# A hybrid decoder trunk on one core: keys and values of the memory as three products of word pairs, and another order at the start, between the layers and at the end

## The chip, the cores and the metric

The kernel runs on one core of a Trainium2 chip. Its time is the device time of one launch in microseconds (us), as the median of several runs. The profile shows one execution. The engines are TensorE (PE, its weight loads PEld), VectorE (DVE), ScalarE (ACT), GpSimd (POOL) and SyncE (SP), which issues most transfers. Each has its own queue of instructions, in program order; they wait for one another by semaphores.

## The reference

Two layers over 512 prompt tokens and 8 single-token samples, 1024 channels, fp32. Each layer normalises `x`, makes one wide projection `h @ w_in`, feeds three branches, and adds `m @ w_out`. The branches are a complex state space (S5), a causal depthwise convolution of 31 taps, and an attention into 256 memory rows. What the change touches is the last one's keys and values, and the norms:

```python
def mem_kv(mem, g, w_k, w_v):
    hm = rmsnorm(mem, g)
    k = (hm @ w_k).reshape(bsz, N_MEM, N_XHEADS, XHEAD_DIM)
    v = (hm @ w_v).reshape(bsz, N_MEM, N_XHEADS, XHEAD_DIM)
    return k, v

h = rmsnorm(x, p['norm_g'])                       # each layer
s_new = ...                                       # powers of exp(lam * dt), a scan over positions
prob = softmax(q k^T * scale); o_x = prob @ v
x = x + m @ p['w_out']
...
y_prompt = rmsnorm(xp, final_norm_g); y_sample = rmsnorm(xs, final_norm_g)
```

## The kernel before

The tokens lie along the free axis: `xT` holds 8 tiles of 128 channels by 520 columns (512 tokens and 8 samples, in two halves of 260). A wide product is not made in fp32. Each operand is split in two fp32r words, a high one and the rest, and three matmuls of 260 columns are added up in PSUM (`split_product`, L785): w_hi by h_hi, w_lo by h_hi, w_hi by h_lo. SP loads the weights in half-units into four slots `w_st`; ACT casts a slot to `w_hi` (L1209), POOL subtracts it from the raw weights to make `w_lo` (L658). A layer has 72 units, in a fixed order: `v0`, `v1`, `q0`, `q1` and so on up to `out`. `first_pair` (L813) makes the first two units together, since it takes each tile of `h` as it comes.

The order on every engine is written out by hand. At the head of a layer DVE makes `ht` from `xT`, the gain and `rs`; ACT casts it to `h_hi` (L1249); DVE subtracts to make `h_lo` (L1692). `rs` is 1/rms as a row over all partitions. In layer 0 it comes from diagonal matrices `dg` that DVE makes (L1668) and PE multiplies by ones (`row_factors`, L755). In layer 1 DVE sums the squares of the new `x` tiles (`add_square`), PE sums over the channels (`square_sums`, L836), DVE takes a reciprocal (L1687), ACT a root.

The keys and values are `key_values`: fp32 matmuls of 128x512, 32 a layer, of the raw weights `wkv` (3 places, loaded two row tiles at a time) and the normalised, gained memory `memg` (L828). Their outputs lie in `mp`; ACT copies the keys to `ktok` and PE turns them to `kT`. They are made in pieces between the turns of the tokens in layer 0, and around `first_pair` in both layers.

Meanwhile DVE computes powers of the state matrix, many operations of 128x16 (`step_factors`, `first_powers`, `chunk_powers`; helper lines L1540, L1556), and then starts the taps of the convolution (`convolution`, first row L1735). Among these it serves the attention: `scores_max` (L1716), and the probabilities' scaling by the reciprocal of their sum (L1723 and `pr<-pr,stat`), for one quarter of the tokens at a time. PE turns the first quarter's probabilities (L709, `mp<-ident,pr`) amid its products; this is the first place behind the layer's head at which PE needs DVE's late work. `state_turns` turn the sample states and the C matrices; DVE copies them to `s0` and `cT` (L1704, L1706).

The end of the program, behind the last product: PE turns `xT` back to rows, ACT squares them with a sum, DVE takes the reciprocal, ACT the root, DVE scales the rows from PSUM by that and the gain row `grow`, SP stores them.

Of the kernel before, what the change touches and what calls it, by code (L numbers as in the profile page):

```python
# [15 lines left out]
F32 = mybir.dt.float32  # L16
# [56 lines left out]
def build(nc, x_prompt, x_sample, mem_prompt, state_ssm_re, state_ssm_im, state_conv, cache_mem_k,  # L73
# [12 lines left out]
    with ctx:  # L86
# [8 lines left out]
        w_dir = sb("w_dir", [P, 2, 12 * P])  # L95
        q = sb("q", [P, ET, 2, HC])
# [6 lines left out]
        dcol = sb("dcol", [P, 4])  # L103
# [37 lines left out]
        def rr(name, off, shape):  # L141
# [13 lines left out]
        drow = ur("drow", 1024, [4, P])  # L155
        dtrow = ur("dtrow", 1040, [80, 2])

# [11 lines left out]
        memg = rr("memg", 6272, [P, KT, MEM])  # L169
# [16 lines left out]
        dg = zr("dg", 2048, [P, 4, P])  # L186
        dgs = zr("dgs", 2560, [NB, NB])
        sq = rr("sq", 0, [P, KT, 2, HC])
        ht = rr("ht", 9216, [P, 2, 2, HC])
        rs = rr("rs", 10256, [P, 2, HC])  # L190
# [33 lines left out]
        grow = rr("grow", 8320, [P, D])  # L224
        ysr = rr("ysr", 9344, [NB, D])
        xsc = rr("xsc", 10368, [P, KT, NB])

# [22 lines left out]
            x_in0 x_in1 xs_in mem_in consts x_tr x_ev dg_done rs_done mem_nrm mem_ev mem_out g_in fin_tr  # L250
            row_sq row_var row_rt fin_y fin_out""".split()}
# [8 lines left out]
            rstd_done=1 ht_done=8 hhi_done=8 h_done=8 par_tr=3 par_ev=3 memg_done=8  # L260
            kv_used=8 kv_ev=2 kT_tr=1 kT_ev=1 kv_out=32 q_ev=4 dt_exp=1 sin_arg=1 par_act=1 sc_done=4
# [73 lines left out]

        block = ctx.enter_context(nc.Block())
# [3 lines left out]
        def _(sp):  # L340
            def param_loads(l):
# [13 lines left out]
                sp.dma_start(drow[:, :], ssm_d[l].rearrange("(q x) -> q x", x=P)).then_inc(sm["p_in"], 16)  # L355
# [27 lines left out]
            for l in range(LAYERS):  # L383
# [20 lines left out]
                def kv_load(i):  # L404

                    src = (w_k, w_v)[i // 4][l].rearrange("(k p) c -> p k c", p=P)
                    if i >= 3:
                        wait(sp, l, "kv_used", i - 2)
# [3 lines left out]
                if l:  # L412
                    kv_load(0)
                    kv_load(1)
                pair("v0")
                if l:
                    kv_load(2)
                else:
                    state_loads(0)
                    kv_load(3)  # L420
                pair("v1")
                for i in range(3 if l else 4, 6):
                    kv_load(i)
                half("q0", 0)
                kv_load(6)
                half("q0", 1)
                kv_load(7)
                half("q1", 0)

# [185 lines left out]
                for j in range(KT):  # L615
# [7 lines left out]
                    if j == 2:  # L623
                        residual_load(1)

# [6 lines left out]
            sp.dma_start(grow[:, :], final_norm_g.rearrange("(o d) -> o d", o=1).to_broadcast([P, D])).then_inc(sm["g_in"], 16)  # L632
# [11 lines left out]
        def _(pool):  # L644
# [7 lines left out]
            for l in range(LAYERS):  # L652
# [49 lines left out]
                for n in range(unit["tail"], UNITS):  # L702
                    low(l * UNITS + n)
# [1406 lines left out]
```

## Time and profile before

| | before |
|---|---|
| time, median of 3 runs | 1102.6 us (1098.14 to 1104.03) |
| the profiled execution | 1097.4 us, of which the span is 1095.6 us |
| mean granted clock of TensorE | 0.990 |
| PE busy | 1057.8 us, 97% of the span |
| DVE busy | 804.3 us, 73% |
| ACT busy | 439.4 us, 40% |
| POOL busy | 405.0 us, 37% |

The span reaches from the first instruction to the last. Busy times are sums over instructions, and the ends of matmuls are modelled, so that rows of PE overlap: a matmul's row is a good deal longer than the step to the next one. What counts is where each engine waits, and for whom; the shares above say nothing of that.

### The profile page before, as it was taken

The numbers are of one execution on the slowest core, as the hardware profiler recorded it, in microseconds if no ns is written. First come the engines' busy times: TensorE is split into PE (matmuls) and PEld (weight loads), VectorE is DVE, ScalarE is ACT, GpSimd is POOL, SyncE is SP. The second block draws the span as 40 slices with busy tenths as digits, with TensorE's granted clock in tenths as the row PEclk, the third lists the DMA queues.
The fourth block names the chain that finished last, engine by engine and source line by source line (L and its number), as shares of the span: only waits on it lengthen the run. The fifth ranks groups of instructions, "written<-read, shape, count | busy, mean of one in ns | idle before, by whom it ended". The sixth has DMA issues, their size and how long they took to land.

```text
span 1095.6 us, 20431 instructions
## 1 busy us (share of the span) xinstructions
PE 1057.8 (97%) x8226; PEld 989.5 (90%) x8226; DVE 804.3 (73%) x1221; ACT 439.4 (40%) x825; POOL 405.0 (37%) x329
## 2 busy tenths in 40 slices
PE   6899999999999999999999999999999999999995
PEld 3669998989999989999966999898999998999994
DVE  3899879898988784444588987989898978544413
ACT  5333653435453352222433355334446346222222
POOL 0135443343342324444412544344443332344440
PEclk8999999999999999999999999999999999999998
DMA  9336519973326933444532562696442694344422
GB/s 266 99 97 173 193 51 206 249 190 98 116 60 152 221 105 120 133 131 159 152 117 78 155 215 67 145 293 171 121 128 59 140 181 148 117 127 136 136 78 78
DMA packets 225268, 155.01 MB, mean 141 GB/s; under 512 B 48650, under 2 KB 201674, under 8 KB 223110
## 3 DMA queue, kind: packets, MB, share of 16 engines
q1 hardware_dynamic: 219318, 141.52, 47.4%
q10 hardware_dynamic: 5856, 12.19, 3.4%
q8 instruction: 65, 1.06, 0.4%
q14 instruction: 29, 0.24, 0.1%
HBM read 130.38 MB, written 24.24 MB: 141 GB/s over the span
## 4 chain that ended last, share of the span: by engine, by line
PE 78%; DVE 11%; DMA 4%; ACT 3%; issue 2%; SPq 1%; POOL 1%; DVEq 0%; ACTq 0%
PE acc L785 54%; PE mp L1132 11%; PE mp L828 3%; PE mp L709 2%; PE mp L1037 1%; PE mp L1005 1%; PE mp L1030 1%; PE mp L896 1%; PE mp L934 1%; DMA w_st<-in_w_br_xatt 1%; DVE br_lo L1814 1%; DVE br_hi L1813 1%; PE acc L813 1%; DVE ht L1546 1%; DVE tiny L1540 1%
## 5 line engine op out<-in xcount | busy, mean ns | idle before, releaser
L658 POOL TENSOR_TENSOR w_lo<-w_st,w_hi 128x512 fp32r<-128x512 f32 x288 | 385.8, 1344 | 608.9 <-ACT w_hi L1209 605.4
L785 PE MATMUL acc<-h_hi,w_hi 128*128 128x260 f32 x1600 | 457.9, 286 | 0.0
L785 PE MATMUL acc<-h_hi,w_lo 128*128 128x260 f32 x1600 | 451.9, 282 | 0.0
L785 PE MATMUL acc<-h_lo,w_hi 128*128 128x260 f32 x1600 | 451.6, 282 | 0.0
L1209 ACT CAST w_hi<-w_st 128x512 fp32r<-128x512 f32 x288 | 178.0, 622 | 358.7 <-PE acc L785 191.2
L785 PEld LDWEIGHTS acc<-h_hi,w_hi 128*128 128x128 f32 x1600 | 301.1, 188 | 7.2 <-issue 3.6
L785 PEld LDWEIGHTS acc<-h_hi,w_lo 128*128 128x128 f32 x1600 | 301.3, 188 | 0.7 <-issue 0.5
L785 PEld LDWEIGHTS acc<-h_lo,w_hi 128*128 128x128 f32 x1600 | 301.4, 188 | 0.0
L1546 DVE SCALAR_TENSOR_TENSOR acc<-vx,cw,acc 128x512 f32<-128x512 f32 x240 | 181.4, 756 | 9.8
L1132 PE MATMUL mp<-br_hi,w_hi 128*128 128x260 f32 x384 | 78.0, 284 | 5.2 <-DVEq L2016 5.2
L1132 PE MATMUL mp<-br_lo,w_hi 128*128 128x260 f32 x384 | 77.4, 283 | 0.0
L1132 PE MATMUL mp<-br_hi,w_lo 128*128 128x260 f32 x384 | 77.2, 283 | 0.0
L785 PE MATMUL acc<-m_hi,w_hi 128*128 128x260 f32 x256 | 69.7, 282 | 0.0
L785 PE MATMUL acc<-m_hi,w_lo 128*128 128x260 f32 x256 | 69.6, 282 | 0.0
L785 PE MATMUL acc<-m_lo,w_hi 128*128 128x260 f32 x256 | 69.6, 282 | 0.0
L1540 DVE TENSOR_TENSOR mj<-mp,xT 128x520 f32<-128x520 f32 x16 | 11.2, 700 | 76.7 <-PE mp L1132 75.8
L1132 PEld LDWEIGHTS mp<-br_hi,w_hi 128*128 128x128 f32 x384 | 59.2, 188 | 6.1 <-issue 6.0
L828 PE MATMUL mp<-wkv,memg 128*128 128x512 f32 x128 | 61.5, 635 | 2.5 <-DVE memg L1640 2.3
L1132 PEld LDWEIGHTS mp<-br_hi,w_lo 128*128 128x128 f32 x384 | 59.3, 188 | 0.0
L1132 PEld LDWEIGHTS mp<-br_lo,w_hi 128*128 128x128 f32 x384 | 59.2, 188 | 0.0
L828 PEld LDWEIGHTS mp<-wkv,memg 128*128 128x128 f32 x128 | 25.2, 203 | 33.0 <-issue 30.0
L1540 DVE TENSOR_TENSOR X<-X,s 128x16 f32<-128x16 f32 (+9 forms) x88 | 51.5, 585 | 3.0
(305 smaller groups left out, 1392.9 us busy)
## 6 DMA issues: line engine op xcount, KB each, us to landing
w_st<-in_w_in SPq DMA_DIRECT2D x208, 256.0 KB, 3.2
g_scratch<-xT ACTq DMA_DIRECT2D x32, 260.0 KB, 2.3
xT<-g_scratch SPq DMA_DIRECT2D x8, 1040.0 KB, 7.4
kb<-in_cache_mem_k SPq DMA_DIRECT2D x16, 512.0 KB, 4.6
kb<-in_cache_mem_v SPq DMA_DIRECT2D x16, 512.0 KB, 6.8
w_st<-in_w_out SPq DMA_DIRECT2D x32, 256.0 KB, 2.8
x_scratch<-xT SPq DMA_DIRECT2D x2, 2080.0 KB, 8.5
xT<-x_scratch SPq DMA_DIRECT2D x4, 1040.0 KB, 5.6
```

What stands on the lines that cost most here:

```text
L658: pool.tensor_tensor(w_lo[:, slot, :], w_st[:, slot, :], w_hi[:, slot, :].bitcast(F32), ALU.subtract).then_inc(w_staged_free, 1)
L709: return pe.transpose(out, in_, ident[0:n, 0:n])
L785: last = pe.matmul(bank(l, i + b), w[:, slot, kk * P:(kk + 1) * P], x[:, k, b, :], start=(k == 0 and p == 0), stop=(k == KT - 1 and p == 2))
L813: last = pe.matmul(bank(l, 2 * i + a), w[:, c % SLOTS, kk * P:(kk + 1) * P], x[:, k, a, :], start=(k == 0 and p == 0), stop=(k == KT - 1 a ...
L828: last = pe.matmul(mp[:, 2 * (1 - i // 4) + m, :], memg[:, k, m * P:(m + 1) * P], wkv[:, i % 3, kk * E:(kk + 1) * E], start=(k == 0), stop ...
L896: last = pe.matmul(mp[:, 2 * (i % 2) + hd // 2, (hd % 2) * MEM:(hd % 2 + 1) * MEM], q[:, hd, i // 2, (i % 2) * P:(i % 2 + 1) * P], kT[:, h ...
L934: last = pe.matmul(mp[:, hd, :], vtok[:, m, hd * P:(hd + 1) * P], pT[:, hd, m, :], start=(m == 0), stop=(m == 1))
L1005: last = pe.matmul(mp[:, 2 * h + e, (r % 4) * YC:(r % 4 + 1) * YC], wl[:, r, e, :], U[:, f * QH + r, e, NB:UC], start=True, stop=True)
L1132: last = pe.matmul(mp[:, 2 * jj + a, 0:HC], w[:, slot, c0:c0 + P], y[:, x, k, a, :], start=(k == 0 and i == 0), stop=(k == ET - 1 and i == 2))
L1209: act.copy(w_hi[:, c % SLOTS, :], w_st[:, c % SLOTS, :]).then_inc(w_hi_done, 1)
L1540: run(dve.tensor_tensor(out, a, b, op), behind)
L1546: run(dve.scalar_tensor_tensor(out=out, in0=a, scalar=s, in1=b, op0=op0, op1=op1), behind)
```

## The change

**Keys and values.** `memg` becomes two words, `mg_hi` (DVE in layer 0, ACT in layer 1) and `mg_lo` (DVE, `memory_low`). The weights become two words a row tile: `key_high` on ACT makes the high word in one of three places `wk[l][n % 3]`, when the products have left it, and `key_low` on POOL the low one. `key_values` counts 16 blocks n of one row tile, with 6 matmuls of 512 columns each, fp32r. **Order.** `state_turns` move from before `first_pair` to between the halves of `v1`, and their copies on DVE behind the first convolution call. `dg` is made by ACT. `step_factors` of layer 0 move behind the h words; `first_powers((1, 2))` of layer 1 move from output unit 6 to behind the last square sum. There are three `ht` buffers, and no wait for the end of each operation in that loop. ACT's `sines(0)` stand before the h casts. **End.** The final gain is a column scale by ACT on `xT` tiles (`gained`); the turns of finished tiles (`final_turns`) stand inside the output units of layer 1, five a unit; ACT keeps raw rows; the squares are summed by PE (`square_rows`); DVE scales rows 0 to 2, ACT row 3 and the samples; ACT issues some of the stores.

```diff
                 def key_values(first, end):
-                    for i in range(first, end):
-                        wait(pe, l, f"d_loaded{i % 3}", 16 * (i // 3 + 1))
-                        for kk in range(2):
-                            k = 2 * (i % 4) + kk
-                            wait(pe, l, "memg_done", k + 1)
-                            for m in range(2):
-                                last = pe.matmul(mp[:, 2 * (1 - i // 4) + m, :], memg[:, k, m * P:(m + 1) * P],
-                                                 wkv[:, i % 3, kk * E:(kk + 1) * E], start=(k == 0), stop=(k == KT - 1))
+                    for n in range(first, end):
+                        k = n % KT
+                        wait(pe, l, "memg_done", k + 1)
+                        wait(pe, l, "wk_done", n + 1)
+                        if l and n == KT:
+                            wait(pe, l, "var_done", 1)
+                        for m in range(2):
+                            for p, (x, w) in enumerate(((mg_hi, 0), (mg_lo, 0), (mg_hi, 1))):
+                                last = pe.matmul(mp[:, 2 * (1 - n // KT) + m, :], x[:, k, m * P:(m + 1) * P],
+                                                 wk[l][n % 3][:, w, :], start=(k == 0 and p == 0), stop=(k == KT - 1 and p == 2))
                         last.then_inc(sm["kv_used"], 1)
...
+            def key_high(l, first, end):
+                for n in range(first, end):
+                    if n % 2 == 0:
+                        wait(act, l, f"d_loaded{n // 2 % 3}", 16 * (n // 6 + 1))
+                    if n >= 3:
+                        wait(act, l, "kv_used", n - 2)
+                    act.copy(wk[l][n % 3][:, 0, :], wkv[:, n // 2 % 3, (n % 2) * E:(n % 2 + 1) * E]).then_inc(sm["wk_hi_done"], 1)
...
+                def key_low(first, end, l=l):
+                    for n in range(first, end):
+                        wait(pool, l, "wk_hi_done", n + 1)
+                        pool.tensor_tensor(wk[l][n % 3][:, 1, :], wkv[:, n // 2 % 3, (n % 2) * E:(n % 2 + 1) * E],
+                                           wk[l][n % 3][:, 0, :].bitcast(F32), ALU.subtract).then_inc(sm["wk_done"], 1)
...
                 if l == 0:
-                    key_values(0, 1)
+                    wait(pe, 0, "par_ev", 1)
+                    key_values(0, 2)
                     token_turns(0)
                     token_turns(1)
                     sample_turns()
-                    key_values(1, 2)
+                    key_values(2, 4)
                     token_turns(2)
                     token_turns(3)
-                    key_values(2, 3)
+                    key_values(4, 6)
                     row_factors()
-                    key_values(3, 4)
+                    key_values(6, 8)
                     pe.wait_ge(sm["x_ev"], 5)
+                    key_values(8, 10)
                 else:
-                    key_values(0, 2)
+                    key_values(0, 4)
                     square_sums()
-                    key_values(2, 4)
-                state_turns()
+                    key_values(4, 12)
                 first_pair()
-                wait(pe, l, "par_ev", 3)
-                key_values(4, 8)
+                key_values(12 if l else 10, 16)
...
-                pair("v1")
+                one("v1", 0)
+                state_turns()
+                one("v1", 1)
...
-                            first_powers((1, 2))
+                            for k in range(KT):
+                                memory_low(l + 1, k, memn[:, k, :])
...
                     dve.sem_inc(sm["sq_sum"], 1)
+                    first_powers((1, 2))
```

On POOL at the seam between the layers, before, the weight words run on with nothing of the keys among them (`w_lo` are the low words of the weights):

```order
L658 TENSOR_TENSOR w_lo<-w_st,w_hi 128x512 x96
L678 MEMSET qrow 40x512
L658 TENSOR_TENSOR w_lo<-w_st,w_hi 128x512 x4
L670 TENSOR_TENSOR vx<-vx,sg 128x4x64 x2
L672 TENSOR_TENSOR v_s<-v_s,sg 128x8
```

Now sixteen subtractions of key words begin there, of which six are shown (the three `wk_` names are the three places):

```order
L668 TENSOR_TENSOR w_lo<-w_st,w_hi 128x512 x94
L690 TENSOR_TENSOR wk_10920_75<-wkv,wk_10920_75 128x512
L690 TENSOR_TENSOR wk_11944_76<-wkv,wk_11944_76 128x512
L690 TENSOR_TENSOR wk_5120_77<-wkv,wk_5120_77 128x512
L690 TENSOR_TENSOR wk_10920_75<-wkv,wk_10920_75 128x512
L690 TENSOR_TENSOR wk_11944_76<-wkv,wk_11944_76 128x512
L690 TENSOR_TENSOR wk_5120_77<-wkv,wk_5120_77 128x512
L668 TENSOR_TENSOR w_lo<-w_st,w_hi 128x512 x2
```

Blocks 0 to 5 of the keys went ahead of the last two weight words of the first pair; ten more blocks stand behind these two.

On DVE at the same place, before, the powers `pw` lie ahead of the last residual adds (`xT<-acc,xT`), and `rs` comes straight behind the last square sum:

```order
L1540 TENSOR_TENSOR pw<-pw 128x16x2
L1540 TENSOR_TENSOR pw<-tiny,pw 128x16x2
L1556 COPY pw<-tiny 128x16x2
L1540 TENSOR_TENSOR xT<-acc,xT 128x260 x2
L1540 TENSOR_TENSOR sq<-sq 128x520 x2
L69 ISA
L1543 TENSOR_SCALAR rs<-mp 128x520
L1687 RECIPROCAL rs<-rs 128x520
```

Now the eight `mg_lo` lie ahead of the adds, and the powers (14 operations, of which the first three and the last three are shown) between the sum and `rs`:

```order
L1772 SCALAR_TENSOR_TENSOR mg_lo<-memn,vec,mg_hi 128x256 x8
L1673 TENSOR_TENSOR xT<-acc,xT 128x260 x2
L1673 TENSOR_TENSOR sq<-sq 128x520 x2
L1673 TENSOR_TENSOR tiny<-pw 128x16 x2
L1673 TENSOR_TENSOR tiny<-tiny 128x16
```

```order
L1673 TENSOR_TENSOR pw<-pw 128x16x2
L1673 TENSOR_TENSOR pw<-tiny,pw 128x16x2
L1689 COPY pw<-tiny 128x16x2
L69 ISA
L1676 TENSOR_SCALAR rs<-mp 128x520
L1825 RECIPROCAL rs<-rs 128x520
```

The powers moved from ahead of `x`'s last tiles to between the last square sum and `rs`.

On ACT ahead of the h casts of layer 0, before (`tiny` are the sines' arguments):

```order
L1165 ACT_TABLE_LOAD
L1165 ACTIVATE tiny<-tiny 128x16
L1166 ACT_TABLE_LOAD
L1166 ACTIVATE tiny<-tiny 128x32
L1209 CAST w_hi<-w_st 128x512 x4
L1249 CAST h_hi<-ht 128x520 x8
```

and now, behind `dg`:

```order
L1282 ACTIVATE dg<-ident,stat 128x128 x4
L1283 ACTIVATE dgs<-ident,stat 8x8
L1245 CAST wk_0_72<-wkv 128x512
L1245 CAST wk_2048_73<-wkv 128x512
L1290 CAST w_hi<-w_st 128x512 x2
L1245 CAST wk_3072_74<-wkv 128x512
L1290 CAST w_hi<-w_st 128x512 x2
L1245 CAST wk_0_72<-wkv 128x512
L1230 ACT_TABLE_LOAD
L1230 ACTIVATE tiny<-tiny 128x16
L1231 ACT_TABLE_LOAD
L1231 ACTIVATE tiny<-tiny 128x32
```

Key casts, each of which waits for PE to leave a place, went between the weight casts, and the sines with their table loads behind them. Five more key casts stand at and among the h casts.

## Rows read from the trace of the kernel before

**Rows 1.** TensorE between the layers: start, us, line, operation, [idle before <-releaser].

```profile
552.70 7.03 PE L828 MATMUL mp<-wkv,memg 128*128 128x512 f32 x16
560.47 1.14 PE L836 MATMUL mp<-sq,ones 128*128 128x260 f32 x4 [0.74 <-DVEq L2062]
```

**Rows 2.** Windows: length, busy of PE PEld DVE ACT POOL, PEclk, DMA, GB/s.

```profile
36.00:40.00 4.00, 4.00 (x12) 2.07 (x11) 2.74 (x14) 0.00 (x0) 0.00 (x0) 0.64 0.93 272
540.00:550.00 10.00, 10.00 (x86) 10.00 (x86) 8.42 (x21) 6.15 (x12) 5.13 (x4) 1.00 0.42 129
```

**Rows 3.** TensorE's timeline in layer 0, where dg arrives.

```profile
35.28 1.13 PE L755 MATMUL acc<-dg,ones 128*128 128x128 f32 x8 [3.16 <-DVEq L1670]
...
36.88 5.40 PE L828 MATMUL mp<-wkv,memg 128*128 128x512 f32 x8
```

**Rows 4.** VectorE's timeline, small operations of the powers, layer 0's last units.

```profile
546.54 1.23 DVE L1540 TENSOR_TENSOR tiny<-tiny,vec 128x16 f32<-128x16 f32 x1
547.80 0.18 DVE L1540 TENSOR_TENSOR tiny<-pw,vec 128x16 f32<-128x16 f32 x1
```

**Rows 5.** GpSimd's timeline at the same place.

```profile
546.45 2.71 POOL L658 TENSOR_TENSOR w_lo<-w_st,w_hi 128x512 fp32r<-128x512 f32 x2 [1.11 <-ACT w_hi L1209]
```

**Rows 6.** VectorE's groups by line and form: count, busy, mean ns, idle.

```profile
L1540 DVE TENSOR_TENSOR mj<-mj,tj 128x520 f32<-128x520 f32 x32 | 42.8, 1337 | 5.8 <-DVE tj L1540 2.9
...
L1540 DVE TENSOR_TENSOR mj<-mp,xT 128x520 f32<-128x520 f32 x16 | 11.2, 700 | 76.7 <-PE mp L1132 75.8 <-DVE mj L1540 0.4 <-DVE br_lo L1814 0.4
```

**Rows 7.** VectorE's timeline in layer 0, up to the convolution's first row.

```profile
30.36 4.59 DVE L1668 TENSOR_SCALAR dg<-ident,stat 128x128 f32<-128x128 f32 x4
...
39.60 0.70 DVE L1682 COPY rs<-acc 128x520 f32<-128x520 f32 x1 [0.85 <-DVE tiny L1540]
...
52.68 1.55 DVE L1692 TENSOR_TENSOR h_lo<-ht,h_hi 128x520 fp32r<-128x520 f32 x2
54.37 0.42 DVE L1704 COPY s<-mp 128x256 f32<-128x256 f32 x1
...
73.06 0.19 DVE L1735 COPY v_last<-vx 128x32 f32<-128x32 f32 x1
```

**Rows 8.** ScalarE's timeline in layer 0, a table load and the first h cast.

```profile
27.81 1.28 ACT L1166 ACT_TABLE_LOAD   x1
...
41.19 0.63 ACT L1249 CAST h_hi<-ht 128x520 fp32r<-128x520 f32 x1 [9.78 <-DVEq L1699]
```

**Rows 9.** VectorE's timeline in layer 1: rs, and the convolution's first row.

```profile
561.65 0.70 DVE L1543 TENSOR_SCALAR rs<-mp 128x520 f32<-128x520 f32 x1 [1.29 <-PE mp L836]
...
596.17 0.19 DVE L1735 COPY v_last<-vx 128x32 f32<-128x32 f32 x1
```

**Rows 10.** TensorE's timeline: kT's and the probabilities' turns in both layers.

```profile
70.81 1.04 PE L709 MATMUL mp<-ident,ktok 128*128 128x128 f32 x8
...
127.19 1.03 PE L709 MATMUL mp<-ident,pr 128*128 128x128 f32 x8
...
596.50 1.04 PE L709 MATMUL mp<-ident,ktok 128*128 128x128 f32 x8
...
653.20 1.03 PE L709 MATMUL mp<-ident,pr 128*128 128x128 f32 x8
```

**Rows 11.** VectorE's timeline: the probabilities of head 0 in both layers.

```profile
124.78 1.22 DVE L1540 TENSOR_TENSOR pr<-pr,stat 128x1024 f32<-128x1024 f32 x1
...
650.79 1.23 DVE L1540 TENSOR_TENSOR pr<-pr,stat 128x1024 f32<-128x1024 f32 x1
```

**Rows 12.** VectorE's waits, 73 to 126 us, then 597 to 652: total, times, longest.

```profile
DVE stat L1723 <- ACT pr L1322: 0.3, 1, 0.3
...
DVE stat L1716 <- PE mp L896: 2.6, 2, 1.7
DVE stat L1723 <- ACT pr L1322: 1.3, 1, 1.3
```

**Rows 13.** VectorE's timeline at the end: the last residual add.

```profile
1076.46 0.43 DVE L1540 TENSOR_TENSOR xT<-acc,xT 128x260 f32<-128x260 f32 x1 [2.35 <-PE acc L785]
```

More of the change, by code:

```diff
@@ L624, in _ @@
                         residual_load(1)
+                    if j == 5 and l + 1 < LAYERS:
+                        wait(sp, l, "sfin_out", 64)
+                        for i in range(3):
+                            kv_load(i, l + 1)
                 wait(sp, l, "kv_out", 32)
@@ L758, in row_factors, with turn_samples, final_turns, square_rows @@
                 last.then_inc(sm["rs_done"], 1)
+            def turn_samples(k):
+                if k == HK:
+                    pe.wait_ge(sm["fin_kept"], HK + 1)
+                if k == KT - 1:
+                    pe.wait_ge(sm["fin_g"], KT + 2)
+                transpose(mp[0:NB, 2, (k % HK) * P:(k % HK + 1) * P], xsc[:, k, :], P).then_inc(sm["fin_tr"], 1)
+            def final_turns(k):
+                if k >= 2:
+                    pe.wait_ge(sm["fin_kept"], rows_kept(k - 2))
+                for i in range(4):
+                    if k < KT - 1 and i == 0:
+                        pe.wait_ge(sm["fin_g"], k + 1)
+                    if k == KT - 1 and i % 2 == 0:
+                        pe.wait_ge(sm["fin_g"], KT + i // 2)
+                    last = transpose(mp[:, k % 2, i * P:(i + 1) * P], xg[:, k % 2, i // 2, (i % 2) * P:(i % 2 + 1) * P], P)
+                last.then_inc(sm["fin_tr"], 1)
+                if k < KT - 1:
+                    turn_samples(k)
+            def square_rows(part):
+                wait(pe, LAYERS - 1, "sq_sum", part + 1)
+                for i in range(4):
+                    last = pe.matmul(mp[:, 3, 4 * i:4 * i + 4], sq[:, part * (KT - 1), i // 2, (i % 2) * P:(i % 2 + 1) * P],
+                                     ones[:, 0:4], start=(i == 0 and part == 0), stop=(i == 3 and part == 1))
+                if part:
+                    last.then_inc(sm["rs_done"], 1)
+            def sample_squares():
+                wait(pe, LAYERS - 1, "sq_sum", 3)
+                pe.wait_ge(sm["fin_kept"], rows_kept(KT - 2))
+                pe.matmul(mp[0:NB, 0, 0:4], sqs[:, :], ones[:, 0:4], start=True, stop=True).then_inc(sm["rs_done"], 1)
             memory_turns(0)
+            param_turns(0)
             memory_turns(1)
-            param_turns(0)
-            wait(pe, 0, "par_ev", 1)
             for l in range(LAYERS):
@@ L1202, in _ @@
             act.wait_ge(sm["row_rt"], 2)
-            sines(0)
+            act.wait_ge(sm["consts"], 3)
+            for i in range(4):
+                act.activation(dg[:, i, :], ident[:, :], ACT.Copy, scale=stat[:, 16 + i:17 + i])
+            act.activation(dgs[:, :], ident[0:NB, 0:NB], ACT.Copy, scale=stat[0:NB, 20:21]).then_inc(sm["dg_done"], 1)
+            key_high(0, 6, 7)
             for l in range(LAYERS):
@@ L1633, in add_square, with memory_low @@
                 tt(sq[:, 0, :, :], sq[:, 0, :, :], sq[:, k, :, :], ALU.add)
+            def memory_low(l, k, rows):
+                wait(dve, l, "mg_hi_done", k + 1)
+                dve.scalar_tensor_tensor(out=mg_lo[:, k, :], in0=rows, scalar=vec[:, 56 + k:57 + k], in1=mg_hi[:, k, :].bitcast(F32),
+                                         op0=ALU.mult, op1=ALU.subtract).then_inc(sm["memg_done"], 1)
             run(dve.memset(stat[:, 4:5], 1.0))
@@ L1665, in _ @@
             dve.sem_inc(sm["x_full"], 1)
-            dve.wait_ge(sm["row_rt"], 1)
-            for i in range(4):
-                run(dve.tensor_scalar(dg[:, i, :], ident[:, :], stat[:, 16 + i:17 + i], None, ALU.mult), behind=1)
-            run(dve.tensor_scalar(dgs[:, :], ident[0:NB, 0:NB], stat[0:NB, 20:21], None, ALU.mult))
-            dve.sem_inc(sm["dg_done"], 1)
-            step_factors(0)
             steps.clear()
```

259 lines of the change are left out of this document (166 added, 93 removed).

## The prediction

> **What bounds the kernel now.** The core's one granted clock is 0.990, so TensorE (PE) runs at 2.4 GHz almost throughout, and the place to start is its timeline at the seams between phases. Between the layers the last product is followed at once by the first half of the keys, 16 records in 7.03 us; the square sums behind them wait 0.74 us for VectorE (DVE) [rows 1]. So PE has hardly a gap there, and the key and value matmuls are time on the path. The windows give the pace of the split products: 86 matmuls of 260 columns in 10.00 us, 0.116 us each, at clock 1.00 [rows 2]. An fp32 matmul of the keys leaves two records, so it takes 2 x 0.44 = 0.88 us.
>
> Then I read what hands PE its work. Ahead of the first products of layer 0 PE idles 3.16 us for `dg`, and the same eight records then take 5.40 us and not 8 x 0.44 = 3.5: the windows show the granted clock at 0.64 there, that is, mostly at the 1.2 GHz level [rows 2, 3]. An idle PE costs twice: its gap, and here 1.8 us behind it.
>
> **A price the argument rests on.** GpSimd (POOL) subtracts words in ops of two SBUF inputs, two in 2.71 us. One DVE op of 128x16 that begins beside them takes 1.23 us; the one behind it takes 0.18 [rows 4, 5]. The groups by form say it of large ones: DVE's `mj<-mj,tj`, both inputs in SBUF, means 1.337 us, and `mj<-mp,xT` of the same size with one in PSUM 0.700 [rows 6]. So a POOL subtraction that meets DVE's two-input work costs DVE 1.23 - 0.18 = 1.05 us; I take 1.0, since some begin in gaps. The Trainium skill, "SBUF — State Buffer", section "Who interferes with whom", has it as an exclusive lock held for the whole instruction, whose loser fully blocks. The trace agrees in kind, and is a little cheaper in size; with a whole op lost each time the sum below would come out some 8 us later.
>
> **The change, part by part.**
> *The products.* 32 fp32 matmuls of 512 columns a layer (32 x 0.86 = 27.5 us; 7.03 / 8 = 0.88 with the ends) become 96 of fp32r. A 512-column one is not in the trace. From 0.116 for 260 columns it is 0.229, from half of a record of 0.43, 0.215; I take 0.22, 21.2 us. PE's work falls by 6.3 us a layer, if it is fed.
> *What feeds them.* Each of 16 blocks a layer now needs an ACT cast (0.6) and a POOL subtraction (1.3) before it, three in flight. POOL can supply a block each 1.3 us, and PE uses one in 6 x 0.22 = 1.3: no reserve. In layer 0 my ordering of the queues by these durations gives: keys end early, but blocks 8 and 9 come at 36.3 and 41.1, so PE idles there; the first pair of products runs from 42.5; block 15 ends at 63.1; `v1` starts at 64.0, where before it starts behind `kT` turns at 70.81 + 0.8 = 71.6 [rows 10]. PE is 7.6 us early.
> *DVE, layer 0.* `dg` goes to ACT (four scalings 4.59 us off DVE), `step_factors` goes behind the h words, so `rs` is copied at 30.3 and not 39.60 [rows 7]. But the h casts wait for ACT, which has key casts, weight casts and now both sines with their table loads of 1.28 us ahead of them: first `h_hi` at 36.5, before 41.19 [rows 8]. With the key casts put between them, the h words end at 52.9 (before 52.68 + 1.55 = 54.2), -1.3. Then: the two state copies moved away -1.1 (0.42 for the first, whose rows are half as long as the second's); `step_factors` now here +3.7; three and a part of a fourth POOL key subtraction (blocks 12 to 15), which now stand among powers, where POOL was idle or had only weight words, +3.4. The convolution, whose first op is `v_last` at 73.06 [rows 7], starts at 77.8: +4.7.
> *DVE, layer 1.* The square sum is complete at 560.4 as before, but `first_powers` now stands between it and `rs`. It is 14 small ops, 14 x 0.21 = 2.9 us, and eight POOL ops (key blocks 3 to 8 and two weight words) fall on it: +8.4. `rs` begins at 571.7, before 561.65 [rows 9]: +10.0. In the h loop the end-of-op waits are gone (-2.0), but ACT's key casts stand between the h casts and five POOL ops meet the words, +5.1: the h words end at 593.6. In the powers behind: copies gone -1.1, blocks 14 and 15 +2.0, and one weight word more +1.4. Sum 10.0 - 2.0 + 5.1 + 2.3 = +15.4: convolution at 611.6, not 596.17 [rows 9]. PE idles 5.3 us for the words (570.6 to 575.9), and enters `v1` 6.6 us later than before (`kT` turns at 596.50 [rows 10]).
> *Where they meet.* PE does not need the convolution itself, it needs what DVE does among it: the turn of the probabilities of head 0, PE 127.19 and 653.20 [rows 10]. DVE has them at 124.78 + 1.22 = 126.0 and 650.79 + 1.23 = 652.0 [rows 11]: 1.2 us ahead in each layer. Between the convolution's start and there DVE's waits are 0.3 us in layer 0, and in layer 1 2.6 for scores and 1.3 for the exponentials [rows 12]; a late DVE finds these done, so its slack is 1.5 us in layer 0 and 1.2 + 3.9 = 5.1, less 0.2 that a shifted PE still leaves, 4.9, in layer 1. The state copies now stand in that stretch (+1.2 with their waits). So at the meeting PE is moved by the larger of its own shift and DVE's:
> layer 0: max(-7.6; 4.7 + 1.2 - 1.5) = **+4.4**;
> layer 1: max(+6.6; 15.4 + 1.2 - 4.9) = **+11.7**.
> PE, 12 us ahead of DVE in layer 0 and 5 in layer 1, idles that long; each gap is followed by slow clock, as at 36.88, +1.8 each [rows 3].
> *State turns* between the halves of `v1`: the same six transposes, 0.6 us, at another place: 0. What waits on them (DVE's copies) is counted above; if they come late, the queue behind is the second convolution, whose cover is the same slack.
> *The key loads of layer 1* come at output unit 5, hidden behind 8 us of products; without that cover key 0 would start some 3 us later. Its real gate is POOL's words: 555.4 against 552.70 [rows 1]; DVE is what is late, so 0 more.
> *The end.* From the last add (1076.46) to the span's end, 1095.6, are 19.2 us [rows 13]. After: add 0.4, gain 0.4, turns 0.5, raw copies 1.2, mean and root 1.0, scaling 0.7, then output transfers of about 8 plus 2.3 to the end: 14.5, -4.7. The turns go into the output units: 35 x 0.1 (eight take 1.03 with their tail [rows 10]) = +3.5, while the products wait. **-1.2**.
>
> **Sum.** 1097.4 (the profiled execution) + 4.4 + 1.8 + 11.7 + 1.8 - 1.2 = 1115.9. The median of the runs shown is 5.2 above that execution; which of them a new kernel falls near is open, I add half: **1118**.
>
> **The rivals.** 0.5%, about what a measurement of this kernel can tell from no change, is 5.5 us.
> *Faster: POOL's added ops cost DVE nothing,* because they fall beside ops that read PSUM or in waits. For it speaks that of the small ops at 546.5 only some are hit [rows 4]. Against: each of them begins while POOL is continuously at work. Then layer 0 has the convolution at 64.7 + 8, and PE's gain is kept: -8.7; layer 1 has it at 593.0, -6.9 at the meeting. 1097.4 - 8.7 - 6.9 - 1.2 = 1080.6, with 2.6: 1083. It decides from a price under about 0.3 us an op. Chance 0.26.
> *No change:* half the price (0.5 an op), 15 ops less 7 in layer 1, PE and DVE level in layer 0: within 5.5 us of before. 0.10.
> *The change doesn't do what it says:* a 512-column fp32r matmul takes 0.43 and not 0.22. 192 x 0.21 = 40 us more PE, of which the 12 and 5 us of idle hide half: 1140. The pace of 260 columns [rows 2] speaks against it. 0.04.
> *My forecast,* DVE late by the POOL ops: 0.60, its own range 1108 to 1130 (14 to 30 ops at 0.7 to 1.05, the meeting's slack by 2 us).
>
> **How the numbers follow.** The range takes in the fast rival's centre and the forecast's upper end: 1083 to 1130; outside lie half of the fast one (0.13), the slow one (0.04) and the forecast's tail (0.03). Faster by over 0.5% 0.26, within 0.10, slower 0.64.
>
> **What would show it.** Of the changed kernel: DVE's `rs` of layer 1 near 571.7, its predecessors of 128x16 with several at 1.2 us; the convolution's first op at 77.8 and 611.6 (each less whatever that layer's start is off by); PE idle some 12 us before the probabilities' turn in layer 0 and 5 in layer 1, with the granted clock low behind; and a 512-column matmul of 0.22. If the small ops stay at 0.2 beside POOL's new ones, the forecast is wrong and the time is the fast rival's. It is wrong too if DVE's stretch from convolution to probabilities shortens by more than 2 us, or if ACT's casts, and not DVE, are what the h words wait for.

## The result, and the profile after

The changed kernel takes 1125.0 us (median of 4 runs, 1124.5 to 1128.7) and the kernel before 1102.8: a ratio of 1.0223, 95% interval 1.0202 to 1.0243. It is slower, as forecast, by 22 us where the forecast had 15, and the time lies inside the range of 1083 to 1130. The profiled execution is the slowest of the four, 1128.7 us with a span of 1126.9; before it was 1097.4 with 1095.6. So the traces differ by 31.3 us of span, some 9 us more than the medians.

TensorE's busy time on the page of the changed kernel:

```profile
PE 1057.9 (94%) x8308; PEld 1013.3 (90%) x8308; DVE 839.2 (74%) x1238; ACT 470.9 (42%) x889; POOL 456.4 (41%) x361
```

It was 1057.8 us before. The sum says little of the work, since TensorE's rows overlap and are longer at the lower clock; but the share of the span fell from 97% to 94%. What is new is waiting. TensorE's waits over the whole span (for whom, us in total, times, longest):

```profile
PE mp L739 <- DVEq L1861: 15.9, 2, 9.9
PE mp L897 <- POOL wk L690: 12.8, 7, 3.8
...
PE mp L897 <- DVE rs L1825: 5.3, 1, 5.3
...
PE mp L965 <- DVE cT L1889: 2.7, 1, 2.7
```

The second are the key words, for which TensorE waits in both layers. The third is in layer 1: the values' first block (block 8) writes to the banks that hold the square sum, and waits until `rs` has been made of it. The fourth is in layer 0, `cT` ahead of the scores. The first is the turn of the probabilities, for which TensorE did not wait before [rows 10, 11]. TensorE's timeline there, in layer 0 and in layer 1:

```profile
137.72 1.97 PE L739 MATMUL mp<-ident,pr 128*128 128x128 f32 x8 [9.92 <-DVEq L1861]
...
682.04 1.97 PE L739 MATMUL mp<-ident,pr 128*128 128x128 f32 x8 [6.02 <-DVEq L1861]
```

They stand at 137.72 and 682.04, where they stood at 127.19 and 653.20 [rows 10]. VectorE is what is late: its timeline of layer 0, `rs`, the last h words, and the first row of the convolution, which stood at 73.06 [rows 7]:

```profile
35.32 0.70 DVE L1820 COPY rs<-acc 128x520 f32<-128x520 f32 x1 [2.73 <-PE acc L788]
...
53.67 1.48 DVE L1830 TENSOR_TENSOR h_lo<-ht,h_hi 128x520 fp32r<-128x520 f32 x2
...
84.72 0.19 DVE L1871 COPY v_last<-vx 128x32 f32<-128x32 f32 x1
```

And in layer 1: the 14 operations of `first_powers` begin at 576.93, then `rs`, then the convolution's first row:

```profile
576.93 2.33 DVE L1673 TENSOR_TENSOR tiny<-pw 128x16 f32<-128x16 f32 x2
579.29 1.19 DVE L1673 TENSOR_TENSOR tiny<-tiny 128x16 f32<-128x16 f32 x1
580.51 1.24 DVE L1673 TENSOR_TENSOR tiny<-pw 128x16 f32<-128x16 f32 x1
...
584.29 1.22 DVE L1689 COPY pw<-tiny 128x16 f32<-128x16 f32 x1
...
587.07 0.22 DVE L1673 TENSOR_TENSOR tiny<-tiny 128x32 f32<-128x32 f32 x1
...
588.35 0.70 DVE L1676 TENSOR_SCALAR rs<-mp 128x520 f32<-128x520 f32 x1
...
628.20 0.19 DVE L1871 COPY v_last<-vx 128x32 f32<-128x32 f32 x1
```

GpSimd's timeline beside those powers, three key words, two weight words, three key words without a pause:

```profile
576.18 4.26 POOL L690 TENSOR_TENSOR wk<-wkv,wk 128x512 fp32r<-128x512 f32 x3 [0.80 <-ACT wk L1245]
580.41 2.54 POOL L668 TENSOR_TENSOR w_lo<-w_st,w_hi 128x512 fp32r<-128x512 f32 x2
582.92 3.78 POOL L690 TENSOR_TENSOR wk<-wkv,wk 128x512 fp32r<-128x512 f32 x3
```

Here the forecast's mechanism can be read off. While GpSimd subtracts, each operation of 128x16 takes 1.17 to 1.24 us, the copy at 584.29 with its one input as well; the one at 587.07, when GpSimd has just stopped, takes 0.22. The 14 operations last from 576.93 to 588.20, 11.3 us, and were forecast at 2.9 + 8.4.

The 31.3 us of span, by the shift of like instructions between the two traces, TensorE's turns and the last adds: +10.5 at the probabilities of layer 0 (137.72 - 127.19); +5.9 from there to the end of VectorE's square sum of layer 1 (576.78 against 560.35), of which 1.9 come before the next quarter's turn; +12.4 from there to the probabilities of layer 1 (28.8 - 16.4); +6.8 to the last residual add (1112.06 against 1076.46 [rows 13], 35.6); -4.3 behind it. The windows around the two turns (length, busy of PE PEld DVE ACT POOL, PEclk, DMA, GB/s) show what an idle TensorE costs behind its gap:

```profile
127.00:137.00 10.00, 0.80 (x7) 0.59 (x5) 9.21 (x14) 2.82 (x12) 0.00 (x0) 0.73 0.27 116
137.00:142.00 5.00, 4.28 (x21) 4.28 (x22) 4.68 (x7) 4.86 (x12) 2.51 (x2) 0.52 0.14 41
682.00:687.00 5.00, 4.96 (x23) 4.96 (x24) 4.61 (x7) 4.36 (x8) 2.51 (x2) 0.50 0.20 57
```

TensorE has idled 9.9 us ahead of the second window and 6.0 ahead of the third; in them its granted clock is 0.52 and 0.50, the 1.2 GHz level. The end, VectorE's last residual add and its three scalings of rows:

```profile
1112.06 0.43 DVE L1673 TENSOR_TENSOR xT<-acc,xT 128x260 f32<-128x260 f32 x1 [1.96 <-PE acc L852]
...
1115.33 2.08 DVE L2228 TENSOR_SCALAR yrow<-yrow,stat 128x1024 f32<-128x1024 f32 x3
```

From 1112.06 to the span's end are 14.8 us; they were 19.1.

### The profile page after: what moved, and what is told of

The parts are those of the page before. It is cut to its first block and busy times, and to the rows that moved or that the text cites. A ratio compares the mean times of both kernels' runs of the same rounds, so it can differ in the third digit from the quotient of the medians.

```text
span 1126.9 us, 20716 instructions
## 1 busy us (share of the span) xinstructions
PE 1057.9 (94%) x8308; PEld 1013.3 (90%) x8308; DVE 839.2 (74%) x1238; ACT 470.9 (42%) x889; POOL 456.4 (41%) x361
## 5 line engine op out<-in xcount | busy, mean ns | idle before, releaser
L668 POOL TENSOR_TENSOR w_lo<-w_st,w_hi 128x512 fp32r<-128x512 f32 x288 | 391.8, 1365 | 573.8 <-ACT w_hi L1290 571.2
L690 POOL TENSOR_TENSOR wk<-wkv,wk 128x512 fp32r<-128x512 f32 x32 | 45.7, 1440 | 57.7 <-ACT wk L1245 57.4
L897 PE MATMUL mp<-wk,mg_hi 128*128 128x512 f32 x128 | 49.6, 451 | 18.2 <-POOL wk L690 12.8
L897 PEld LDWEIGHTS mp<-wk,mg_hi 128*128 128x128 f32 x128 | 27.6, 216 | 28.6 <-issue 22.3
```

The costliest lines, as they stand in the source:

```text
L668: pool.tensor_tensor(w_lo[:, slot, :], w_st[:, slot, :], w_hi[:, slot, :].bitcast(F32), ALU.subtract).then_inc(w_staged_free, 1)
L690: pool.tensor_tensor(wk[l][n % 3][:, 1, :], wkv[:, n // 2 % 3, (n % 2) * E:(n % 2 + 1) * E], wk[l][n % 3][:, 0, :].bitcast(F32), ALU.subtr ...
L897: last = pe.matmul(mp[:, 2 * (1 - n // KT) + m, :], x[:, k, m * P:(m + 1) * P], wk[l][n % 3][:, w, :], start=(k == 0 and p == 0), stop=(k ...
```

## The experiments

All times are medians, with the kernel before measured beside them on the same chip (1101.0, 1101.5 and 1101.7 us in the three groups). The changed kernel's 1125.0 is from another group, with 1102.8 beside it, so that a difference from it is sure to 1 or 2 us only. The theory: a GpSimd subtraction blocks VectorE's work of two SBUF inputs, VectorE comes late to the probabilities, and TensorE waits there. The rivals: the order of VectorE's work is what costs; or the feeding of the products does.

**The suspected cost alone, in the kernel before.** Behind the first four weight words of a layer GpSimd does 12 operations more, for which nothing waits; in the second kernel they are 24 memsets instead:

```diff
                 pair("v0")
+                for i in range(12):
+                    pool.tensor_tensor(extra[l][:, 1, :], extra[l][:, 0, :], extra[l][:, 0, :], ALU.subtract)...
# the other: for i in range(24): pool.memset(extra[l][:, 1, :], 0.0)...
                 wait(pool, l, "kv_ev", 1)
```

Expected of the subtractions: 

> The kernel before, with 12 extra GpSimd subtractions of 128x512 (two SBUF inputs) a layer, behind the first four weight words of the layer; nothing waits for their result. If such an operation blocks VectorE's two-input work (some 1.0 us each): in layer 0 all 12 meet powers and h words, 12 less 1.5 of slack, +10; in layer 1 some 8 meet the h words, 8 less 4.9, +3 to +7; together 1115 to 1120. If GpSimd's work costs VectorE nothing: 1102.6, within 0.5%.

Expected of the memsets: 

> The same place and about the same time of GpSimd, but 24 memsets a layer, which read nothing. If what costs is that GpSimd reads SBUF beside VectorE: within 0.5% of 1102.6. If it is any work of GpSimd there (its queue, its writes): as slow as the subtractions, 1115 or more.

Measured: 1113.1 us with subtractions (ratio 1.0112, 1.0084 to 1.0140) and 1101.7 with memsets (1.0008, 0.9996 to 1.0021). GpSimd's and VectorE's timelines with the subtractions, a small operation and an `ht`:

```profile
35.75 14.17 POOL L681 TENSOR_TENSOR extra<-extra 128x512 f32<-128x512 f32 x12
```

```profile
38.22 0.90 DVE L1546 TENSOR_TENSOR tiny<-tiny 128x16 f32<-128x16 f32 x1
...
47.73 1.30 DVE L1552 SCALAR_TENSOR_TENSOR ht<-xT,vec,rs 128x520 f32<-128x520 f32 x1 [0.16 <-DVE ht L1552]
```

And with the memsets, GpSimd's row and the same two operations of VectorE:

```profile
35.44 13.95 POOL L681 MEMSET extra<- 128x512 f32 x24
```

```profile
37.32 0.18 DVE L1546 TENSOR_TENSOR tiny<-tiny 128x16 f32<-128x16 f32 x1
...
42.53 0.76 DVE L1552 SCALAR_TENSOR_TENSOR ht<-xT,vec,rs 128x520 f32<-128x520 f32 x1 [0.16 <-DVE ht L1552]
```

GpSimd is busy for 14 us in either. With subtractions an operation of 128x16 takes 0.90 and not 0.18, an `ht` 1.30 and not 0.76. The convolution of layer 0 starts at 80.72, with memsets at 74.35. So it is not GpSimd's time that costs, it is what it reads: +12 us for 24 subtractions. Memsets are not free for every operation: a `tensor_scalar` of 128x16, with one input, takes 0.52 us beside them (at 37.82) and 0.17 in the kernel before.

The 12 us are below the 1115 to 1120 that the theory expected: in layer 0 twelve subtractions cost 6.4 us (80.72 less 74.35), 0.5 each and not 1.0. And they do not reach the time at the probabilities, where TensorE does not wait in this kernel. They delay the h words, for which the first products wait, and both engines are late from there on. TensorE's turn of the keys in layer 0, with subtractions and with memsets:

```profile
78.79 1.04 PE L715 MATMUL mp<-ident,ktok 128*128 128x128 f32 x8
```

```profile
72.64 1.04 PE L715 MATMUL mp<-ident,ktok 128*128 128x128 f32 x8
```

So this pair of kernels shows the blocking, and not the meeting at the probabilities.

**The same cost taken out of the changed kernel.** The key words' subtraction becomes two memsets, so the low words of key and value weights are zero, and TensorE still makes all three products:

```diff
-                        pool.tensor_tensor(wk[l][n % 3][:, 1, :], wkv[...], wk[l][n % 3][:, 0, :].bitcast(F32), ALU.subtract)...
+                        pool.memset(wk[l][n % 3][:, 1, :].bitcast(F32), 0.0)...
+                        pool.memset(wk[l][n % 3][:, 1, :].bitcast(F32), 0.0)...
```

Expected: 

> The changed kernel, in which GpSimd writes the low words of the key and value weights by two memsets and not by a subtraction (so the low words are zero; TensorE still makes all three products). GpSimd is busy about as long. If the subtractions block VectorE: the 32 blocks cost about 1.0 us less each, the small operations of layer 1's powers go back to 0.2 us, VectorE's convolution starts some 10 us earlier in each layer, and the time falls to 1095 to 1105. If the order of VectorE's work (powers between sum and rs, step factors behind the h words) or the supply of words is what costs: 1118 to 1125.

Measured: 1100.3 us (0.9992, 0.9976 to 1.0007), 24.7 less than the changed kernel. The same powers on VectorE's timeline, `rs`, and the convolution of layer 1:

```profile
560.42 0.41 DVE L1674 TENSOR_TENSOR tiny<-pw 128x16 f32<-128x16 f32 x2
560.87 0.17 DVE L1674 TENSOR_TENSOR tiny<-tiny 128x16 f32<-128x16 f32 x1
...
565.59 0.70 DVE L1677 TENSOR_SCALAR rs<-mp 128x520 f32<-128x520 f32 x1 [1.75 <-PE mp L906]
...
600.26 0.19 DVE L1872 COPY v_last<-vx 128x32 f32<-128x32 f32 x1 [8.52 <-POOL v_s L682]
```

The small operations take 0.17 to 0.24 us again (only the last copy, at 563.44, takes 0.39), and the 14 of them 3.4 us where they took 11.3. But the time is that of the kernel before, and not the 1083 that my fast rival gave. TensorE's turn in layer 0:

```profile
128.58 1.75 PE L740 MATMUL mp<-ident,pr 128*128 128x128 f32 x7 [6.60 <-DVEq L1862]
```

TensorE still waits 6.6 us there: it is early, and VectorE is not, so the early start of `v1` is worth nothing. In layer 1 the order is turned around, VectorE waits 8.5 us for `v1` (600.26), so that TensorE and what feeds it are late: it waits 2.6 us for `mg_lo` and 1.5 for words. A rival is left by this pair alone: two memsets are done a little sooner than a subtraction, and TensorE's waits for key words over the whole span fall from 12.8 to 7.7 us. The kernels with both pieces of the order back, below, settle it.

**VectorE's order, piece by piece.** Layer 1's first powers back ahead of the last adds; layer 0's step factors back ahead of `rs`, with the sines back ahead of `dg`; and both:

```diff
                         if j == 6:
+                            first_powers((1, 2))
                             for k in range(KT):
                                 memory_low(l + 1, k, memn[:, k, :])
...
                     dve.sem_inc(sm["sq_sum"], 1)
-                    first_powers((1, 2))
# the other: step_factors(0) ahead of rs again, sines(0) ahead of dg
```

Expected of the powers: 

> The changed kernel, with layer 1's first powers back ahead of the last residual adds. By blocking: only three key blocks can be there (three places), so rs comes some 8 us earlier, but most of the other subtractions then meet the h words and the later powers; VectorE is late by nearly as much at the probabilities, 1117 to 1123. If the place of the powers alone is what costs in layer 1 (11 us ahead of rs): 1112 to 1115.

Expected of the step factors: 

> The changed kernel with layer 0's step factors back ahead of rs, and the sines back ahead of dg. TensorE waits some 12 us for VectorE at the probabilities of layer 0. If VectorE's lateness there is what sets the time, the 3.7 us of step factors, now in its wait for rs, come off, less the 3 by which dg is later: -1 to -4 against the changed kernel, 1121 to 1124. If layer 0's lateness is absorbed: 1125.

Expected of both: 

> The changed kernel with real low words and both pieces of VectorE's order back. The powers alone gave -2.6, the step factors -1.2; if they add, 1121. The subtractions stay, so it stays over 1115 by the blocking theory; were the order the cause, it would come near 1100.

Measured: 1122.4 (1.0195, 1.0173 to 1.0217), 1123.8 (1.0204, 1.0181 to 1.0227) and 1120.6 us (1.0172, 1.0143 to 1.0202). Each piece is worth a few us at most, and not all of the 22; the first two intervals overlap that of the changed kernel (1.0202 to 1.0243), and the third touches it. VectorE's timeline with the powers back, `mg_lo` and `rs`:

```profile
569.75 3.26 DVE L1772 SCALAR_TENSOR_TENSOR mg_lo<-memn,vec,mg_hi 128x256 fp32r<-128x256 f32 x8
...
580.28 0.70 DVE L1676 TENSOR_SCALAR rs<-mp 128x520 f32<-128x520 f32 x1 [3.84 <-PE mp L905]
```

`rs` is 8 us earlier than at 588.35, but `mg_lo` now comes behind the powers, and TensorE waits 5.2 us for it. With the step factors back it is these that meet GpSimd:

```profile
35.23 2.48 DVE L1673 TENSOR_TENSOR tiny<-tiny 128x16 f32<-128x16 f32 x2
...
43.06 0.70 DVE L1821 COPY rs<-acc 128x520 f32<-128x520 f32 x1 [0.42 <-DVE tiny L1673]
```

The two operations at 35.23 take 2.48 us. The subtractions find whatever stands in their time, so moving VectorE's work around mostly moves the loss.

**Is it VectorE's lateness at the probabilities?** Six of the 31 taps of the first convolution call are left out in both kernels (the output lacks them), 4.7 us of VectorE a layer:

```diff
                     for k in range(first, end):
+                        if i == 0 and 10 <= k < 16:
+                            continue
```

Expected of the changed kernel: 

> The changed kernel, with 6 of the 31 taps of the first convolution call left out in each layer: 6 x 0.78 = 4.7 us less of VectorE between the convolution's start and the probabilities. In the changed kernel TensorE waits 9.9 us there in layer 0 and 6.0 in layer 1. If VectorE's lateness sets the time in both layers: -9.4, 1115 to 1116. If only the late start of TensorE's own work sets it: 1125.

Expected of the kernel before: 

> The same six taps left out of the kernel before, where TensorE does not wait at the probabilities, and VectorE has them 1.2 us ahead: within 2 us of before, whatever the theory. It is the control for the edit: were it to gain 9 as well, the taps would cost something else than lateness.

Measured: 1114.6 us (1.0118, 1.0089 to 1.0148), 10.4 less than the changed kernel, and 1100.8 (0.9997, 0.9981 to 1.0012). TensorE's turns in the first:

```profile
134.33 1.97 PE L739 MATMUL mp<-ident,pr 128*128 128x128 f32 x8 [8.25 <-DVEq L1861]
...
670.87 1.10 PE L739 MATMUL mp<-ident,pr 128*128 128x128 f32 x8 [0.25 <-DVEq L1861]
```

In layer 1 its wait fell from 6.0 to 0.25 us; in layer 0 it is 8.3 and the turn 3.4 us earlier. The same edit gives nothing where TensorE does not wait. That is the clearest sign of what sets the changed kernel's time: VectorE's lateness at the probabilities, which the first pair of kernels could not show.

**What is left of the products without the blocking and without the moves.** The last two edits together with the memsets:

Expected: 

> The changed kernel with both pieces of VectorE's order back (powers of layer 1 ahead of the last adds, step factors of layer 0 ahead of rs) and the low words by memset (zero). What is left of the change is then TensorE's shorter products, the supply of their words by ScalarE and GpSimd, and the end. If the blocking and the two moves are all that costs: 1083 to 1092. If feeding the blocks (three places, casts and words in step with TensorE) eats the products' gain by itself: 1095 to 1102.

Measured: 1096.6 us (0.9965, 0.9948 to 0.9982), which is the second answer: TensorE waits 7.7 us for the key words in all and 3.7 for `mg_lo`, and the shorter products bring little.

Against the kernel with both pieces back and real low words (1120.6 us) it is 24.0 us less, and there TensorE waits 7.1 us for the key words, no longer than here. So in this order, too, the subtractions cost 24 us, and it is not the supply of the words that costs them.

**The other parts alone, in the kernel before.** First the new end; then with the h loop of the change; then with its state turns as well:

```diff
-        ht = rr("ht", 9216, [P, 2, 2, HC])
+        ht = rr("ht", 8320, [P, 3, 2, HC])
...
-                    run(dve.tensor_tensor(h_lo[:, k, :, :], ht[:, k % 2, :, :], h_hi[:, k, :, :].bitcast(F32), ALU.subtract))
-                    dve.sem_inc(sm["h_done"], 1)
+                    dve.tensor_tensor(h_lo[:, k, :, :], ht[:, k % 3, :, :], h_hi[:, k, :, :].bitcast(F32),
+                                      ALU.subtract).then_inc(sm["h_done"], 1)
```

Expected of the end: 

> The kernel before with the new end alone (gain as a column scale by ScalarE, turns of finished tiles inside the output units, squares summed by TensorE, row 3 and the samples scaled and stored by ScalarE). By the trace of the changed kernel the stretch behind the last residual add is 4.3 us shorter, and the turns cost 35 x 0.1 = 3.5 us among the products, +-1: a net of -1, 1100 against 1101, not to be told from no change. If the turns hide in waits of TensorE for ScalarE or VectorE in the output units: -4. If they cost the clock as well: +1.

Expected with the h loop: 

> The same with the change's h loop too (three ht buffers, no waits for the end of each operation). The h loop of a layer gets 2 us shorter on VectorE where ScalarE's casts allow; in layer 1 the first pair waits for it, so that part reaches the time, and in layer 0 VectorE's lateness at the probabilities is what counts: -2 to -4 against end_only. If the first pair is bound by TensorE itself: within 1 us of end_only.

Expected with the state turns: 

> The kernel before with the new end and the h loop (1093.1), and the state turns between the halves of v1 with VectorE's copies behind the first convolution call, as in the change, but no products of words. If the move is neutral, as counted: within 1 us of 1093. If it takes TensorE's wait for the copies ahead of the keys away: -1 to -2. If the late copies hold the scores up, as the 2.7 us wait of TensorE for cT in the changed kernel suggests: +1 to +3.

Measured: 1098.3 us (0.9972, 0.9960 to 0.9984); **1093.1 us (0.9929, 0.9915 to 0.9943)**; 1095.8 us (0.9944, 0.9926 to 0.9963). The last residual add with the end alone:

```profile
1085.13 0.43 DVE L1615 TENSOR_TENSOR xT<-acc,xT 128x260 f32<-128x260 f32 x1 [1.96 <-PE acc L829]
```

The span ends at 1099.9, 14.8 us behind it, as in the changed kernel. VectorE's timeline with the h loop, layer 1: the first two `ht` without a gap, the convolution:

```profile
564.65 1.43 DVE L1776 SCALAR_TENSOR_TENSOR ht<-xT,vec,rs 128x520 f32<-128x520 f32 x2 [0.70 <-ACT rs L1286]
...
591.24 0.19 DVE L1813 COPY v_last<-vx 128x32 f32<-128x32 f32 x1
```

The convolution starts 4.9 us earlier than before (596.17 [rows 9]) in layer 1, and 2.7 earlier in layer 0 (70.38). The second kernel is the best of all that ran: 8.4 us under the kernel before and 31.9 under the changed one. It has the end and the h loop, and none of the rest. The h loop brings 5.2 us over the end alone, more than the 2 to 4 expected. The late state turns take 2.7 us of it back by the medians, but the intervals overlap (0.9915 to 0.9943, 0.9926 to 0.9963), and the profiled executions are alike: spans of 1092.4 and 1092.1 us.

With these, the kernel of late state turns (1095.8) and the one of zero words (1096.6) differ in the products and the casts, memsets and `mg_lo` that feed them, in `dg` on ScalarE and in the order of loads. The intervals overlap. So the three fp32r products, with their words' price on VectorE taken away, bring nothing over 32 fp32 matmuls that this measurement could tell.

## Why the prediction was right, and where its terms were off

**Blocking, the price that carries the forecast: shown.** In the kernel before by the dose and its control, in the changed one by the removal, in two orders of VectorE's work: 24.7 and 24.0 us go when GpSimd writes without reading. The size of 1.0 us each holds for the powers of layer 1 (eight subtractions, 11.3 us and 3.4); in the dose it is 0.5, so it is no constant. This case's runs also bear the Trainium skill's "SBUF — State Buffer", section "Who interferes with whom", out in a point that the forecast didn't need: a GpSimd operation that only writes does not contend with VectorE's two inputs (memsets, 1.0008).

**The meeting at the probabilities: shown.** The rule max(TensorE's shift; VectorE's shift less its slack) had VectorE as the late one in both layers, and the missing taps gave back 10.4 us where nothing came back in the kernel before.

**TensorE's lead in layer 0, 7.6 us: wrong, and by luck without effect.** Its turn of the keys begins at 67.69, 3.1 us earlier than before (70.81 [rows 10]) and not 7.6, and at the probabilities it stands ready at 127.80 (137.72 less 9.92), 0.6 us later than before. Of the lead 2.7 us went into the wait for `cT`, the copies that the change put behind the convolution, and 0.6 into the state turns themselves, which now stand behind the keys' turn. As VectorE was later still, the larger of the two shifts was not TensorE's, and the miss shows only in the wait, 9.9 us where some 12 were forecast.

**Layer 1: +11.7 forecast, +12.4 in the trace.** The powers' 11.3 us were met to a tenth. From `rs` (588.35) to the convolution (628.20) are 39.9 us; the forecast had 611.6 - 571.7 = 39.9. In that sum two errors cancel: the h words took 20.7 us and not 21.9, the powers behind them 19.2 and not 18.0. TensorE was to idle 5.3 us for words; it idles 6.2 for words and another 5.3 for `rs`, a wait that the forecast didn't have, and is still only 5.6 us late at the keys' turn (forecast 6.6).

**Layer 0: +4.4 forecast, +10.5 in the trace.** The mechanism was right, and two terms of the sum were mis-sized, the end of the h words and the subtractions behind them. First, "`rs` is copied at 30.3": it is copied at 35.32. I let it follow the copies of the tokens, and left out the queues ahead of it. The last tokens are turned 2.4 us later than before, from 29.15, and their copies end at 32.60; ScalarE makes `dg` and `dgs` behind its roots, up to 31.7; and TensorE comes to the row factors only at 33.69, without a gap behind key blocks 4 and 5. TensorE's timeline, the last tokens' turns, the end of block 5, the row factors:

```profile
29.15 1.92 PE L739 MATMUL acc<-ident,xrow 128*128 128x128 f32 x16
...
33.46 0.39 PE L897 MATMUL mp<-wk,mg_hi 128*128 128x512 f32 x1
33.69 1.05 PE L786 MATMUL acc<-dg,ones 128*128 128x128 f32 x8
```

But `rs` is not what the h words wait for, ScalarE is. Its timeline, the sines' last table load and the h casts:

```profile
39.05 1.28 ACT L1231 ACT_TABLE_LOAD   x1
...
40.99 1.15 ACT L1337 CAST h_hi<-ht 128x520 fp32r<-128x520 f32 x2
```

The sines end at 40.6, one key cast follows (three key casts stand at and among the h casts of layer 0, and not five), and the first h cast starts at 40.99 and not at 36.5. VectorE waits 2.1 us for it, so that a sign of being wrong that the forecast named, h words that wait for ScalarE's casts, came true at the first word. The loop makes up for half of it: the h words end at 55.15 and not at 52.9, 2.2 us late. Second, "three and a part of a fourth POOL key subtraction, +3.4". GpSimd's timeline from the end of the h words to the convolution:

```profile
61.66 4.07 POOL L690 TENSOR_TENSOR wk<-wkv,wk 128x512 fp32r<-128x512 f32 x3 [5.50 <-ACT wk L1245]
65.69 5.10 POOL L668 TENSOR_TENSOR w_lo<-w_st,w_hi 128x512 fp32r<-128x512 f32 x4
...
73.79 1.28 POOL L668 TENSOR_TENSOR w_lo<-w_st,w_hi 128x512 fp32r<-128x512 f32 x1 [1.45 <-ACT w_hi L1290]
75.23 1.30 POOL L668 TENSOR_TENSOR w_lo<-w_st,w_hi 128x512 fp32r<-128x512 f32 x1 [0.16 <-ACT w_hi L1290]
80.19 2.71 POOL L668 TENSOR_TENSOR w_lo<-w_st,w_hi 128x512 fp32r<-128x512 f32 x2 [3.66 <-ACT w_hi L1290]
```

There are 11 subtractions of 128x512 there, three of keys and eight of weights, where before there were four. With TensorE early, the weight words of the next units come early too, and a late VectorE has more of them beside its powers: the stretch takes 29.6 us, 8.3 more than the 21.3 of the same work before (17.6 of powers and 3.7 of step factors), and not 3.4. That is 4.9 us. The kernel of zero low words, with the order of the change, has six subtractions of weights in this stretch and takes 24.3 us for it (51.21 to 75.49): 21.3 us with four subtractions, 24.3 with six, 29.6 with eleven. 2.2 and 4.9, less 0.2 for the state copies, make the 6.9 by which the convolution is later than its 77.8; less 0.8 between there and the turn it is the +6.1 at the meeting. The general price had been seen, but the words counted were those of the change alone, not those that the change brings forward.

**Clock, +1.8 at each gap:** 1.9 in layer 0 and 2.7 in layer 1, by the shift of ScalarE's casts behind each turn. **Between the clock's 1.9 us and the square sum of layer 1** 4 us more came up, which the forecast put at nothing. 1.4 of them are VectorE's wait for the cached keys' transfer at the attention of the samples, 4.9 us where it was 3.5; 1.5 come in the last output units of layer 0; and in the window from 230 to 240 the clock is 0.83, where it was 1.00. What delays that transfer no run tells; and since the medians differ by 9 us less than the profiled executions, a part of the 4 may be of this one execution alone. Behind layer 1's turn 6.8 us came up: the clock's 2.7, the end's turns with 3.5, and 0.6 elsewhere.

**The end, -1.2:** the stretch behind the last add became 4.3 us shorter (forecast 4.7), and the turns cost 3.5 by count. Alone it gave -3.3 by the medians (0.9972, 0.9960 to 0.9984). In its trace the last output units grew by 3.6 us (the first add came 5.1 us later than before, the last one 8.7), so the turns hide nothing there, and -0.8 would be left; that execution was the slowest of its eight. Where the medians' other 2.5 us come from is open.

**State turns at 0: neither shown nor refuted.** +2.7 us by the medians without the products, with intervals that overlap; in that kernel TensorE does not wait for `cT`. In the changed kernel it waits 2.7 us for it ahead of the scores. The forecast named that queue and trusted in its cover.

**The h loop** was counted as -2.0 in layer 1 alone, and drowned there. By itself it brought 5 us over both layers, the most of any part. Whether the third buffer or the missing gaps bring it was not tested.

**The fast rival** (1083) was wrong beyond its condition. With the price gone the time was 1100.3, because "PE's gain is kept" doesn't hold: in layer 0 TensorE waits for VectorE anyway, and in layer 1 it waits for `mg_lo` and for words. **The rival that a 512-column fp32r matmul takes two passes** is out: three of them take 577.37 - 576.68 = 0.69 us, 0.23 each, on TensorE's timeline of the changed kernel:

```profile
576.68 0.62 PE L897 MATMUL mp<-wk,mg_hi 128*128 128x512 f32 x2
577.13 0.40 PE L897 MATMUL mp<-wk,mg_lo 128*128 128x512 f32 x1
577.37 0.39 PE L897 MATMUL mp<-wk,mg_hi 128*128 128x512 f32 x1
```

## What to carry to other kernels

Work that one engine takes from another is not free because the engine that takes it over is idle: ask what its operands' reads block, and count every operation of its queue that falls into the blocked stretch, those that the change brings forward too. When TensorE gets faster ahead of a meeting point, look up who arrives last there; if it is another engine, the gain is a longer wait, and a slower clock behind it. Split a bundle before judging it: here one part that was hardly noticed, the h loop, brought more than any other, and the words of keys and values took it all away.

## What the runs showed that was not expected

Twelve GpSimd subtractions a layer that nothing waits for cost 12 us in all, and 24 memsets at the same place 0.7 us, which can't be told from nothing (0.9996 to 1.0021). The h loop with a third buffer and without gaps of some 0.15 us between its operations was worth 5 us over both layers. And the time of a kernel was moved by 10 us by leaving out 9.4 us of an engine whose busy share is 74%.
